# Two transformer layers on one core: weight casts moved ahead of chunk work, a small product moved, gate tiles put first

## The reference, cut to what matters

```python
h = rmsnorm_2(x, norm_mix_g)
qk_ml, v_ml, o_ml, if_pre, q_sw, k_sw, v_sw, g_a, g_b = split(h @ w_in)
qk_ml = silu(causal_depthwise_conv(qk_ml, conv_qk))
h_ml = rms(mlstm_chunkwise(q_ml, k_ml, v_ml, ig, lf)) * mlstm_norm_g
y_a = sigmoid(o_ml) * h_ml
y_b = swa_with_sinks(q_sw, k_sw, v_sw, sinks)
merged = sigmoid(g_a) * (y_a @ w_branch_a) + sigmoid(g_b) * (y_b @ w_branch_b)
x = x + merged @ w_out
x = x + square(relu(rmsnorm_2(x, norm_mlp_g) @ w_up)) @ w_down
gate = sigmoid(rmsnorm_2(x, norm_ple_g) @ w_ple_gate)
x = x + gate * (p @ w_ple_proj)
return rmsnorm_2(x, final_norm_g)
```

## Time and profile before

| what | value |
|---|---|
| median of 3 runs | 2051.27 us (2050.69 to 2051.84) |
| the profiled execution | 2049.75 us, span 2047.9 us |
| mean granted TensorE clock | 0.969 |
| TensorE busy | 1899.2 us, 93% |
| VectorE, ScalarE, GpSimd busy | 897.6, 742.0, 820.9 us |

### The profile page before, as it was taken

How to read it: one execution, slowest core, us unless ns; L and a number is a source line. 1 busy time by engine, 2 the same in 40 slices (tenths; PEclk the granted TensorE clock), 3 DMA queues, 4 the chain that set the end, 5 groups by cost and what they waited for, 6 DMA issues and landing times.

```text
span 2047.9 us, 24253 instructions
## 1 busy us (share of the span) xinstructions
PE 1899.2 (93%) x8988; PEld 1530.5 (75%) x8988; DVE 897.6 (44%) x1324; ACT 742.0 (36%) x1190; POOL 820.9 (40%) x413
## 2 busy tenths in 40 slices
PE   5999999899899999998999969999898999999986
PEld 3786767688788888877677448878786888888865
DVE  5136786601458824863731451126465431032116
ACT  5346776342333222223233332224322432133232
POOL 3244666363034454445233044350033344434431
PEclk9999999999999999999999779999998999999988
DMA  4321000242022233233122002320021222222221
GB/s 146 116 100 41 1 1 29 85 155 103 1 93 99 96 123 120 85 107 123 58 85 99 21 0 82 103 96 8 11 103 64 100 98 91 98 103 85 100 103 41
DMA packets 24116, 162.43 MB, mean 79 GB/s; under 512 B 2800, under 2 KB 3312, under 8 KB 4976
## 3 DMA queue, kind: packets, MB, share of 16 engines
q1 hardware_dynamic: 23040, 159.39, 22.0%
q10 hardware_dynamic: 1008, 2.12, 0.3%
HBM read 159.40 MB, written 2.10 MB: 79 GB/s over the span
## 4 chain that ended last, share of the span: by engine, by line
PE 79%; DVE 9%; POOL 4%; ACT 4%; issue 4%; DMA 0%; DVEq 0%; SPq 0%; ACTq 0%; POOLq 0%
PE psum L451 76%; POOL w_lo L2206 2%; PE psum L753 2%; ACT w_hi_r L1033 1%; POOL q_st L2242 1%; DVE tmp L1644 1%; DVE sqt L1995 1%; ACT spare L1442 1%; DVE tmp L1852 1%; DVE tmp L2158 1%; DMA ring<-in_panels 0%; DVE acc L2003 0%; DVE negmax L2050 0%; DVE h_lo L1800 0%; DVE xt L1603 0%
## 5 line engine op out<-in xcount | busy, mean ns | idle before, releaser
L2206 POOL TENSOR_TENSOR w_lo<-ring,w_hi_r 128x2048 fp32r<-128x2048 f32 x142 | 657.4, 4631 | 989.8 <-ACT w_hi_r L1033 989.7
L451 PE MATMUL psum<-big_r,w_hi_r 128*128 128x512 f32 (+1 forms) x1568 | 479.1, 389 | 33.0 <-DVE big_r L1582 8.7
L451 PE MATMUL psum<-h_hi,w_hi_r 128*128 128x512 f32 x1200 | 473.3, 394 | 20.5 <-POOL w_lo L2206 11.5
L451 PE MATMUL psum<-h_lo,w_hi_r 128*128 128x512 f32 x1200 | 469.7, 391 | 0.0
L451 PE MATMUL psum<-h_hi,w_lo 128*128 128x512 f32 x1200 | 469.4, 391 | 0.0
L1033 ACT CAST w_hi_r<-ring 128x2048 fp32r<-128x2048 f32 x144 | 274.1, 1904 | 285.6 <-PE psum L451 282.8
L451 PEld LDWEIGHTS psum<-big_r,w_hi_r 128*128 128x128 f32 x1568 | 296.9, 193 | 95.0 <-issue 32.9
L451 PE MATMUL psum<-big_r,w_lo 128*128 128x512 f32 (+1 forms) x784 | 303.5, 387 | 0.0
L451 PEld LDWEIGHTS psum<-h_hi,w_hi_r 128*128 128x128 f32 x1200 | 227.0, 189 | 74.4 <-issue 14.4
L451 PEld LDWEIGHTS psum<-h_hi,w_lo 128*128 128x128 f32 x1200 | 226.8, 189 | 47.8
L451 PEld LDWEIGHTS psum<-h_lo,w_hi_r 128*128 128x128 f32 x1200 | 227.2, 189 | 47.2 <-issue 0.5
(11 more groups left out here) (305 smaller groups left out, 2327.0 us busy)
## 6 DMA issues: line engine op xcount, KB each, us to landing
ring<-in_panels SPq DMA_DIRECT2D x148, 1024.0 KB, 4.7
xt<-in_x SPq DMA_DIRECT2D x4, 512.0 KB, 6.5
out<-big SPq DMA_DIRECT2D x8, 256.0 KB, 2.2
big<-in_mem ACTq DMA_DIRECT2D x1, 1024.0 KB, 4.6
q_st<-in_ple ACTq DMA_DIRECT2D x1, 512.0 KB, 3.4
spare<-in_w_gate ACTq DMA_DIRECT2D x1, 192.0 KB, 6.4
spare<-in_w_k ACTq DMA_DIRECT2D x1, 128.0 KB, 8.8
params<-in_params ACTq DMA_DIRECT2D x1, 114.0 KB, 4.9
```

Of the source, the lines that this page charges most:

```text
L451: return nc.tensor.matmul(o, l, r, start=start, stop=stop, **kw)
L2206: g.tensor_tensor(w_lo[:, p], ring[:, p], plain(w_hi[:, p]), ALU.subtract).then_inc(lo_done[j], 1)
```

## The change

Five edits go together. (1) Casts ahead: in `gained` the cast for the next pair goes ahead of the slot's last chunk, except at the stage's last chunk, and in ml_qk ahead of both silus. (2) GpSimd subtracts in the two FFN down stages only the columns in use, 1536 and 1280. (3) The scaling by the first layer's final norm leaves ml_qk's loop and follows behind ml_if's drains. (4) In both merges the first pair runs its two gate tiles first, in banks 0 and 2, and then its two branch tiles, both in bank 1. (5) ple_v moves from behind mlp_down_b to between merge_b and mix_out; its result goes to `spare`, its unused slot 0 is cast and subtracted in 8 columns only, and ple_g becomes a `product_gained` directly behind mlp_down_b. The split of the ple input moves ahead of merge_b on VectorE.

```diff
-    ("sw_q", 2, 4), ("sw_kv", 1, 6), ("merge_b", 4, 4), ("mix_out", 2, 4),
+    ("sw_q", 2, 4), ("sw_kv", 1, 6), ("merge_b", 4, 4), ("ple_v", 1, 8), ("mix_out", 2, 4),
     ("mlp_up_a", 4, 4), ("mlp_down_a", 4, 2), ("mlp_up_b", 4, 4), ("mlp_down_b", 4, 2),
-    ("ple_v", 1, 8), ("ple_g", 2, 4),
+    ("ple_g", 2, 4),
...
             def merge(name, rhs, ready):
+                for j in range(2):
+                    weights_here(name, 0, j)
+                    if j == 0:
+                        bank_free(name, 0, 0)
+                    for k in range(KD):
+                        last = mm3(bank(2 * j), w(j * PANEL + k * P), hk(k), k == 0, k == KD - 1)
+                    last.then_inc(tile_done, 1)
+                pe.wait_ge(*ready)
+                for j in range(2):
+                    bank_free(name, 0, 2 * j + 1)
+                    for k in range(KD):
+                        last = mm3(bank(1), w(j * PANEL + (KD + k) * P), rhs(k), k == 0, k == KD - 1)
+                    last.then_inc(tile_done, 1)
...
             pe.wait_ge(small_split, 6)
-
             weights_here("ple_v", 0, 1)
...
+            pe.wait_ge(split_done, SPLIT0["mlp_a"])
+            product("mix_out", 2, lambda k: (chunk_r(8 + k), chunk_r(24 + k)))
...
+            product_gained("ple_g", 2, "ple2", lambda: token_sums(7, acc), lambda: spread_rows(6, r_tok))
@@ ScalarE, gained @@
+                        for n in tiles_[:-1]:
+                            chunk_of(n)
+                        if tiles_[-1] < KD - 1:
+                            wait_tile(name, i, per // 2 * (j + 1) - 1)
+                            hi(PAIR0[name] + 1 + i, j)
+                            chunk_of(tiles_[-1])
+                        else:
+                            chunk_of(tiles_[-1])
+                            hi(PAIR0[name] + 1 + i, j)
@@ ScalarE, ml_qk @@
+            with loop(act, 2) as i:
+                for j in range(2):
+                    wait_tile("ml_qk", i, 2 * j + 1)
+                    hi(PAIR0["ml_qk"] + 1 + i, j)
+                    for k in range(2 * j, 2 * j + 2):
+                        act.wait_ge(conv_done, FC + k + 1 + 4 * i)
+                        nc.scalar.activation(cols(big, 4 * S * i + k * S), tmp[:, k % 2 * S:(k % 2 + 1) * S],
+                                             ACT.Silu).then_inc(gated, 1)
@@ ScalarE, the merges @@
+                for j in range(2):
+                    sigmoid(0, j)
+                for j in range(2):
+                    wait_tile(name, 0, 2 + j)
+                    hi(PAIR0[name] + 1, j)
...
-            act.wait_ge(ml["y"], 2 * MLH)
-            gate("merge_a")
+            gate("merge_a", (PANEL, PANEL))
...
+            gate("merge_b", (NARROW, PANEL))
+            hi(PAIR0["mix_out"], 0)
+            for c in range(KD):
+                wait_tile("ple_v", 0, c)
+                nc.scalar.copy(spare[:, c * S:(c + 1) * S], bank(c % 2)).then_inc(evac[c % 2], 1)
+            hi(PAIR0["mix_out"], 1)
@@ VectorE, ml_qk and behind ml_if @@
-                    step(V.scalar_tensor_tensor(out=x, in0=x, scalar=params[:, bass.ds(4 * i + k + COL["final"], 1)],
-                                                in1=bank(6), op0=ALU.mult, op1=ALU.mult))
+            for c in range(KD):
+                g0 = COL["final"] + c
+                V.scalar_tensor_tensor(out=xc(c), in0=xc(c), scalar=params[:, g0:g0 + 1], in1=bank(6), op0=ALU.mult,
+                                       op1=ALU.mult)
@@ GpSimd @@
+            low(PAIR0["nsa_out"] + 1, PAIR0["ffn_down_a"] - PAIR0["nsa_out"] - 1)
+            low(PAIR0["ffn_down_a"], 4, (HALF["ffn_a"] * P, HALF["ffn_a"] * P))
+            low(PAIR0["ffn_up_b"], PAIR0["ffn_down_b"] - PAIR0["ffn_up_b"])
+            low(PAIR0["ffn_down_b"], 4, (HALF["ffn_b"] * P, HALF["ffn_b"] * P))
+            low(PAIR0["ml_qk"], PAIR0["merge_a"] + 1 - PAIR0["ml_qk"])
```

More of the change, by code:

```diff
@@ L1407, in _, with gate, sigmoid @@
             y_hi(MLH - 1)
-            def gate(name):
-                def slot(i, j):
+            def gate(name, last):
+                def sigmoid(i, j):
                     act.wait_ge(evac[0], TILE0[name] // 2 + j + 1 + 2 * i)
@@ L1414, in slot @@
                         .then_inc(gate_sig, 1)
-                    wait_tile(name, i, 2 * j + 1)
-                phase(name, 4, slot)
-            act.wait_ge(ml["y"], 2 * MLH)
-            gate("merge_a")
+                for j in range(2):
+                    sigmoid(0, j)
+                for j in range(2):
+                    wait_tile(name, 0, 2 + j)
+                    hi(PAIR0[name] + 1, j)
+                with act.Fori(1, 3) as i:
+                    for j in range(2):
+                        sigmoid(i, j)
+                        wait_tile(name, i, 2 * j + 1)
+                        hi(PAIR0[name] + 1 + i, j)
+                for j in range(2):
+                    sigmoid(3, j)
+                    wait_tile(name, 3, 2 * j + 1)
+                    hi(PAIR0[name] + 4, j, n=last[j])
+            gate("merge_a", (PANEL, PANEL))
             through("sw_q", 2)
@@ L1490, in _ @@
             gained("mlp_down_b", 4, "ple2", gain_of("ple2"))
[L1492 to L1497 removed]
+            root(7, r_tok[:, :], bank(2, NT))
             take_row("ple2", 6)
[L1499 removed]
             def ple_gate(i, j):
@@ L2126, in _, with merge_b @@
             V.tensor_tensor(ple_lo, ple_raw, plain(ple_hi), ALU.subtract).then_inc(small_split, 1)
+            def merge_b(i, j, at_=None):
+                y = tmp[:, j * S:(j + 1) * S]
+                n0 = 2 * S * i + j * S
+                dve.wait_ge(tile_done, TILE0["merge_b"] + (2 * j + 2 + 4 * i if at_ is None else at_))
+                dve.wait_ge(gate_sig, 8 + j + 1 + 2 * i)
+                dve.wait_ge(split_done, sp_.at)
+                V.tensor_tensor(y, bank(1), act_o[:, j * S:(j + 1) * S], ALU.mult).then_inc(evac[1], 1)
+                dve.wait_ge(evac[1], TILE0["merge_b"] // 2 + j + 1 + 2 * i)
+                step(V.tensor_tensor(y, cols(big, n0 + 8 * S), y, ALU.add))
+                settle()
+                split(y, cols(big_r, n0 + 8 * S), cols(big_r, n0 + 24 * S))
+            d0, sp0 = d.n, sp_.n
+            for j in range(2):
+                merge_gate("merge_b", 0, j, 2 * j, j + 1)
+            for j in range(2):
+                merge_b(0, j, j + 3)
+            d.n, sp_.n = d0, sp0
+            with dve.Fori(1, 4) as i:
+                d.enter(i, 4)
+                sp_.enter(i, 2)
+                for j in range(2):
+                    merge_gate("merge_b", i, j)
+                    merge_b(i, j)
+            d.leave(4)
+            sp_.leave(4)
             gained("mix_out", 2, 4, "mlp2", gain_of("mlp2"))
```

121 lines of the change are left out of this document (42 added, 79 removed).

## The result

The changed kernel took 2018.80 us, median of 4 runs (2017.51 to 2020.93), and the kernel before on the same chip 2050.98 (2046.11 to 2051.84): a ratio of 0.9845, 95% interval 0.9833 to 0.9858. The forecast was 2022. On another chip the same two kernels gave 2015.42 and 2051.14, ratio 0.9827 (0.9812 to 0.9842). The profiled execution took 2019.35 us. First the page: the span fell by 30.3 us against the earlier trace rows, and TensorE's busy time only from 1899.2 to 1891.3.

What follows compares the result with a forecast made beforehand. TensorE was taken to carry most of the chain, with gains in its idle times. Terms summed to -30.85, with clock -28.95: 2049.75 profiled became 2020.8, and 1.5 for the median gave 2022; range 2012 to 2034.

Steps and rivals of the forecast that it cites:

- other casts, clock: Other reordered casts: nothing, within 0.5 us; one new short wait probably followed by a slow clock, +1.9 us.
- Down b: Second FFN down stage, part b: refill falls to 5.0 us, no waits left, VectorE's 1.10 goes too; gain 13.1 us.
- The term of -1.0: Start of the first mLSTM product: 1.7 us of slow clock recovered, partly offset by a later accumulation; gain about 1.0 us.
- Query and key stage: mLSTM query and key stage: 5.4 us lost in place of 8.2, with waits at blocked drains; gain 2.8 us.
- rival (2): VectorE escapes GpSimd's blocks, so 4.4 us of waits and the tail's first-chunk blocks go: 2014 us; chance 0.1.
- Merge a: Second gate tile fills the wait for y, 1.5 us stays, slow start mostly goes, new cost 1.25; gain 7.2 us.
- Merge b pays the same 1.25 and hides nothing: Merge b: the new tile order costs 1.25 us and gains nothing, since its y is there in time.
- The moved product: Ple value product between merge b and output product: starts after a 6.65 us refill, costs 10.0 us there.
- The tail: Gate product directly behind the down product, VectorE setting the end with two blocked chunks; gain 18.0 us.
- (1): Each short wait left or added is followed by a 1.9 us slow stretch, seven times: 2033 us; chance 0.15.
- (3): Tail is bound at TensorE by refills and gains only the 8.59 us and its clock: 2031 us; chance 0.07.
- (4): All 27 moved casts delay the chunk's two-input operation by 4.0 us, all reaching TensorE: 2130 us; chance 0.04.

Runs made afterwards that it cites:

- e3: Changed kernel with casts behind the chunk's work again in the five residual stages, short subtractions kept; 2015.67 us in one run.
- e4: Changed kernel with full 2048-column subtractions in both FFN down stages, casts still ahead; 2015.90 us in one run.
- e1: Changed kernel with the ple value product back between the last down product and the gate product; 2024.46 us, ratio to before 0.9887.
- e2: Changed kernel with merge b in its old order, merge a still changed; 2013.33 us, ratio to before 0.9825.
- e6: Changed kernel with each query and key stage cast behind both silus again, final-norm scaling still outside the loop; 2012.14 us in one run.
- e9: Changed kernel with merge a in its old order, merge b still changed; 2022.44 us, ratio to before 0.9875.
- e8: Changed kernel with the ple value product's weights split over both slots instead of all in slot 1; 2010.29 us, ratio to before 0.9806.
- e10: Changed kernel with both casts of the last gate product's first pair ahead of the gate work; 2024.22 us, ratio to before 0.9870.
- e7: Changed kernel with each query and key stage cast between the two silus of its slot; 2015.65 us in one run.
- e5: Changed kernel with casts behind the chunk's work in five residual stages and full 2048-column subtractions; 2031.84 us, ratio to before 0.9918.
- e0: The changed kernel again, unedited, on another chip with a second profile; 2015.42 us.

## Why the prediction was right, point by point

The terms, as forecast and as the table has them, in us:

```
                                        forecast   measured
down b and start of the mLSTM product    -14.1      -13.1
query and key stage                       -2.8       -3.7
merge a (and the attention behind it)     -7.2       -8.5   (-6.5 and -2.0)
merge b                                   +1.25      +2.7
ple value product before mix              +10.0      +9.9
tail                                      -18.0      -18.6
other casts, clock                        +1.9       +1.1   (stages ahead)
sum                                      -28.95     -30.3   (with -0.1 in the mLSTM)
```

The sum is better than its terms. They miss by 0.1 to 1.5 us, 6 us in all, in both directions, and cancel down to 1.35. The last row is luck: +1.9 was for one slow stretch behind a new short wait, and what stands beside it is the drift of the stages ahead, which run 894.5 to 897.8 us with the same code. The attention's -2.0 was in no term. The rest of the distance from 2022 to 2018.80 is in the step from the profiled execution to the median, taken as +1.5, which came out as -0.55.

**Down b.** Right, and with two edits of which each alone does most. The piece of 249 matmuls has no stop, and the wait of 1.10 went. Counted to the stage's end the gain is 13.6 (67.9 to 54.2), forecast 13.1. With a refill of 4.95 us for a half of 6.8 there was room to spare: e3 (later cast) and e4 (full subtraction) lose 3.3 and 2.4 at the same state of the clock, both together 11.5. Either edit brings the refill about to the length of a half; the second adds 2 to 3 us, about half of it outside the stage's own refills: the wait of 1.10 (e4) and the one for the next stage's weights (e3).

**Start of the mLSTM product.** The term of -1.0 failed: it was +0.5. The slow stretch that I had put down to the old wait (1.7) appeared without it, 958.90 to 962.30, with no wait above 0.3 us ahead of it. In e1, e2, e6 and e9 the stage has none with the same code, and the column is 1.6 shorter; there the term would have come as -1.1. And e3 has a wait of 1.80 us there and no slow stretch behind it. So what I had priced as the wait's cost was not the wait's.

**Query and key stage.** The size held roughly (5.4 us lost against streaming were forecast, 48.1 - 43.6 = 4.5 measured), the places did not. The timeline of ScalarE, GpSimd and VectorE, as the earlier trace rows:

```profile
968.25 1.28 ACT L1036 ACT_TABLE_LOAD   x1 [1.78 <-PE psum L452]
969.54 1.92 ACT L1036 CAST w_hi_r<-ring 128x2048 fp32r<-128x2048 f32 x1
...
971.54 4.62 POOL L2255 TENSOR_TENSOR w_lo<-ring,w_hi_r 128x2048 fp32r<-128x2048 f32 x1 [10.34 <-ACT w_hi_r L1036]
...
972.36 4.08 DVE L1668 TENSOR_SCALAR tmp<-q_st,params 128x512 f32<-128x512 f32 x1 [0.15 <-DVE q_st L1661]
...
980.50 6.63 DVE L1670 SCALAR_TENSOR_TENSOR tmp<-q_st,params,tmp 128x511 f32<-128x511 f32 x3
...
981.76 4.82 POOL L2255 TENSOR_TENSOR w_lo<-ring,w_hi_r 128x2048 fp32r<-128x2048 f32 x1 [5.61 <-ACT w_hi_r L1036]
```

I had the first block in chunk 0 and 2.05 us before the fourth tile. A table load of 1.28 us in front of the first cast, which I had left out, put the subtraction just behind chunk 0's last multiply-add. The block fell on chunk 1, whose drain was already through, and TensorE waited 0.33 us before the fifth tile. The next block, at 980.50, held the drain at 987.05 and cost the 2.20 before the sixth. There are four blocks of about 4 us, and only one of them makes TensorE wait for more than 1 us. This was rival (2) for one block and the forecast for another; its 2014 us did not come, because in the tail both blocks fell on VectorE's path. The Trainium skill, "SBUF — State Buffer", section "Who interferes with whom", says that whoever issues first holds the shared ports for the whole instruction and the other is fully blocked. By that rule, the trace agrees: 6.63 us for three operations that take 2.54 without a subtraction, and 4.08 for one that takes 0.49.

**Merge a.** Right in mechanism. The wait is 1.59 us (forecast 1.5), and the first y tile runs at full clock. The bill of 1.25 for the new order came as 0.78 for the drain of the shared bank and 0.22 for the weights. The attention's 2.0, which is clock and went with the same edit in e9, was in no term.

**Merge b.** The step that was mis-sized: "Merge b pays the same 1.25 and hides nothing" is right in sign, and measured 2.7, of which 2.1 go with the order by e2 and 0.5 (88.2 to 88.7) with the clock: the half-clock stretch at the stage's start lies wholly inside it now, 1443.60 to 1447.00. The waits are 0.79 + 0.67 = 1.46; the last 0.6 are open. Some 0.5 of the attention's -2.0 is the other side of this: before has a stretch across merge b's start (1466.2 to 1469.6), and a second one wholly ahead of it (1456.0 to 1459.4) that after does not have.

**The moved product.** Start at 6.66 us (forecast 6.65), mix +9.9 (forecast +10.0). The bound that I took as given, its weights in slot 1, was a layout, and e8 took 7.8 us of it away.

**The tail.** VectorE sets the end, as forecast: a free chunk takes 4.52 us (1996.09 to 2000.61), and two are blocked:

```profile
1971.73 4.49 DVE L2207 TENSOR_TENSOR tmp<-spare,o_acc 128x512 f32<-128x512 f32 x1 [0.93 <-ACT o_acc L1531]
...
1984.87 4.37 DVE L2207 TENSOR_TENSOR tmp<-spare,o_acc 128x512 f32<-128x512 f32 x1 [0.81 <-ACT o_acc L1531]
...
2004.30 0.69 DVE L2211 TENSOR_TENSOR acc<-acc,sqt 128x512 f32<-128x512 f32 x1 [0.69 <-ACT sqt L1535]
```

TensorE's wait of 2.97 us inside it (forecast 3.6) costs next to nothing: behind it VectorE waits for TensorE once, 0.43 us before the drain at 1983.37. That is argued from the profile alone; e10, meant to show it, changed VectorE's path as well and so shows only what a wrong place for the cast costs.

**The other rivals.** (1), a slow stretch behind every short wait, would have been +11; the half-clock stretches seen at new waits are at 1539.20 and in the tail, and the waits of 2.20, 1.59, 0.79 and 0.67 us had none behind them. It is not a law: in e4_full_sub the same wait (2.23 us, before 988.32) was followed by one, and its "qk, v" is 1.6 us longer. The window of e4 behind it:

```profile
989.50:992.90 3.40, 3.40 (x10) 2.63 (x9) 2.88 (x5) 0.63 (x1) 0.00 (x0) 0.50 0.55 229
```

(3) would have shown as some -9 in rest, where -18.6 came. (4), 4 us for each cast, is a danger only where the blocked engine sets the end: in the tail two blocks cost VectorE 3.8 and 3.7 us.

## What to carry to other kernels

A refill that is too long for its cover can be shortened or started earlier; measure each alone, since either may do most of it. Before you put a cast that waits for a later tile ahead of chunk work, look at which engine sets the end of the stage: where it is not TensorE, the work queued behind the cast comes late, and the subtraction that it releases may fall on that engine as well (7.0 us here). Putting independent tiles first fills a wait only where there is one: the same reordering gave 6.5 us in merge a and cost 2.1 in merge b.

## What the runs showed of the hardware

The same code had two lengths in this kernel. The mLSTM's chunkwise part took 82 us or 77 us, its 160 matmuls busy for 64.93 or 58.11 us at a mean granted clock of 0.81 or 0.88. The shorter one came in e3, e4, e6 and e7. These differ from after ahead of the part, but e5 differs there too and has the longer one. They are also all the executions that ran on the third chip, and no profile with the longer one is from that chip, so chip and edit cannot be told apart here. The time at which the part begins does not decide it: 1107.13 us in e10 (82), 1107.36 in e7 (77). Why the slow stretches fall differently is open. The other slow stretch that comes and goes, the one of 1.6 us behind down b, is no matter of the chip: with the same code it is there in e8, e0 and e7 and missing in e1, e2 and e6, one of each on each chip. The lesson is in the size: 5 us is larger than most of the terms here, and not an effect of any edit inside the stage.

A one-input VectorE operation was blocked as fully as the two-input ones: 4.08 us for L1668 (512 columns by a column of scalars) against 0.49 us free.
